# Identity products in TensorE's pauses: 62 at a layer's end, 30 ahead of the norm of the experts

## The chip, the cores and the metric

The kernel runs on one core of a Trainium2 chip. The metric is the device time of one execution in microseconds (us), as the median over runs. The core has TensorE (PE, matrix products into PSUM banks), VectorE (DVE), ScalarE (ACT) and GpSimd (POOL), each with a queue of its own that it works off in order, and SyncE (SP), which issues most of the loads. Engines wait for each other on semaphores. PE's clock is granted in one of two levels, 1.2 and 2.4 GHz; the profile gives it as a share of full speed (PEclk).

## What is computed

The reference is one inference step of a diffusion backbone with two layers, over two groups of tokens with shared weights: 128 context tokens and 256 latent tokens, D = 1024. Cut to what matters here:

```python
def trunk_layer(x, cond, lp_norm, lp_mix, lp_moe, ctx, lam_init):
    mod = jax.nn.silu(cond) @ w_mod_l + b_mod_l
    sh1, sc1, g1, sh2, sc2, g2 = jnp.split(mod[..., None, :], 6, axis=-1)
    h = rmsnorm(x, norm_mix_l) * (1.0 + sc1) + sh1
    y, new = mixer_sublayer(h, lp_mix, ctx, lam_init)   # four mixers, gated merge, output projection
    x = x + g1 * y
    h = rmsnorm(x, norm_ffn_l) * (1.0 + sc2) + sh2
    x = x + g2 * hier_moe(h, *lp_moe)                   # top-1 group of 4, top-2 of its 4 experts
    return x, new
```

After the two layers comes a last rmsnorm. All weights and tokens are float32.

## The kernel before

The 384 tokens stand in three tiles of 128. Each engine has its own instruction stream, and each stream holds one loop over the two layers (`with pe.Fori(0, DEPTH) as l`), whose body walks a list of steps written out ahead of time (SCHEDULE). A layer is: the norm ("norm", 0) with the first units of the input projection; the units of the projections, with the steps of the mixers laid between them; the output projection (wout); the norm of the experts ("norm", 1); the router ("route"); and the experts ("experts"), a loop over six tiles of sorted tokens.

Weights come in units of 512 KB (128 x 1024 f32) through a ring of raw buffers. Each unit is split into a high and a low part in fp32r (whi by ACT, wlo by DVE or POOL), and every product is made of three: high x high, low x high, high x low (function three, L1271 to L1273). The activations are split the same way into hhi and hlo.

The norm. ACT sums the squares of each tile (L952), POOL makes the reciprocal root (L758, L762), DVE and ACT scale the tokens into xn (L1798, L961). PE then transposes xn column by column, 128 of the 1024 features at a time and three tiles to a column (function columns, L1293), DVE applies the modulation while it reads the bank (L1826), ACT makes the high part (L968), DVE and POOL in turn the low part (L1746, L775). In the norm of the experts PE also transposes the finished columns back (function back, L1335) and ACT stores them in hn (L956). Of the first norm, four columns stand ahead of unit 0 and two each behind units 0 and 1. DVE's stream has the low part of unit 0's weights behind the first column, ahead of the low part of the first column.

Ahead of the norm of the experts PE works a quad (function next_quad, L1230): 32 products that make part of the modulation of the next layer. The second quad stands behind the last column, then the router.

At a layer's end the outputs of the last tile of experts are brought back to the tokens' order (back_to_tokens, L1683) and added to x by DVE (L1746); the next layer's sum of squares waits for that (layer_end).

S, T, G and O are PSUM tensors; S has two banks, S0 and S1. The function free(bank) waits until the last reader of a bank is through; a matmul without a wait of its own starts when PE comes to it.

Of the kernel before, what the change touches and what calls it, by code (L numbers as in the profile page):

```python
# [28 lines left out]
P = 128  # L29
# [62 lines left out]
ROPE_AFTER = (20, 21, 22, 22, 23, 43, 45, 47, 49)  # L92
BIASED = [u for u, (ty, t, j) in enumerate(AU) if ty in "BC" and t < 2]
SMALL = 36
FOUR = ("T0", "T1", "S0", "S1")

# [140 lines left out]
def program(nc, a, out, counts):  # L238

    ctx = ExitStack()  # L240
    with ctx:
        def sb(name, shape, dt=F32):
            return ctx.enter_context(nc.sbuf_tensor(name, shape, dt))
# [44 lines left out]
        cst, nrow = sig[:, 2, :], sig[0:1, 0:2, :]  # L288
        small = sb("small", [P, KD, SMALL])
        smhi = sb("smhi", [P, KD, SMALL], F32R)  # L290
        smlo = sb("smlo", [P, KD, SMALL], F32R)
        pcol = sb("pcol", [P, PCOLS])
# [7 lines left out]
        ident = sb("ident", [P, P])  # L300
# [64 lines left out]
        S = ctx.enter_context(nc.psum_tensor("S", [P, 2, 512], F32))  # L365
# [8 lines left out]
        def rows_bank(i, j):  # L374

            return ("S0", "S1", "S0", "S1")[j] if i == 0 else FOUR[j]

        def psum(name):

            return {"S": S, "T": T}[name[0]][:, int(name[1]), :]  # L380
# [76 lines left out]
        def evacuated(c, t):  # L457
            if CHUNKS[c][0] in ("proj", "gate"):
                return ev_act, TILES * sum(CHUNKS[i][0] in ("proj", "gate") for i in range(c)) + t
            step = 2 if c == CHUNK_NO["wout", 1] else 1  # L460
            return ev_dve, TILES * sum(CHUNKS[i][0] not in ("proj", "gate") for i in range(c)) + step * t
# [5 lines left out]
        def pooled(c, t):  # L467

            n = sum(CHUNKS[i][0] == "wout" or (CHUNKS[i][0] == "branch" and CHUNKS[i][1][0] > 0) for i in range(c))
            return TILES * n + t  # L470
# [414 lines left out]
        def _(act):  # L885
# [6 lines left out]
            with act.Fori(0, DEPTH) as l:  # L892
# [46 lines left out]
                for s in SCHEDULE:  # L939
# [213 lines left out]
                    elif s[0] == "mt":  # L1153
                        c = s[1]
                        act.wait_ge(*mt_pe.at(l, c))
                        mh_act.of(nc.scalar.activation(hhi[:, c, :], psum(FOUR[c % 4])[:, 0:384], ACT.Copy, scale=0.5))
                    elif s == ("route",):
# [63 lines left out]
        def _(pe):  # L1221
# [5 lines left out]
            def next_quad(q, where, signal):  # L1227
                for k in range(KD):
                    for i in range(MQ):
                        mm = nc.tensor.matmul(G[32 * i:32 * i + 32, q // 2, P * (q % 2):P * (q % 2 + 1)], cond[:, k, :],  # L1230
                                              where[MQ * q + i][:, k * P:(k + 1) * P], start=(k == 0), stop=(k == KD - 1))
                        if k == KD - 1:
                            signal(mm)
# [15 lines left out]
            with pe.Fori(0, DEPTH) as l:  # L1249
                passed = {}  # L1250

                def need(s, i):

                    if i > passed.get(s.name, -1):
                        passed[s.name] = i
                        pe.wait_ge(s.handle, s.value(l, i))
# [4 lines left out]
                def free(*banks):  # L1261
                    last = {}
                    for b in banks:
                        if read[b] is not None:
                            sgl, i = read[b]
                            last[sgl.name] = (sgl, max(i, last.get(sgl.name, (sgl, i))[1]))
                    for sgl, i in last.values():
                        need(sgl, i)
# [7 lines left out]
                def quad(q):  # L1276
                    need(nx_in[q], MQ - 1)
                    next_quad(q, home, nx_pe.of)

                def turned(h):  # L1280
# [3 lines left out]
                    nxt_pe.of(next_turned(h))  # L1284
                    read["T0"] = None

                def columns(w, c):

                    b = ("T0", "T1") if w else ("T0", "T1", "S0", "S1")
                    b = b[c % len(b)]  # L1290
                    free(b)
                    for t in range(TILES):
                        mm = nc.tensor.transpose((T if b[0] == "T" else S)[:, int(b[1]), t * P:(t + 1) * P],  # L1293
                                                 xn[:, t, c * P:(c + 1) * P], ident[:, :])
                    nt_pe.of(mm)
                    read[b] = (hf_dve, KD * w + c)

                pe.wait_ge(*yo_act.in_tile(l, 0, 1, -1))
                for s in SCHEDULE:
                    if s[0] == "mod":  # L1300
# [11 lines left out]
                        for k in range(KD):  # L1312
                            for q in range(MQ):
                                mm = nc.tensor.matmul(O[32 * q:32 * q + 32, c0:c0 + P], cond[:, k, :],  # L1314
                                                      raw[:, MODPOS[j - MQ + 1 + q] % RAW, k * P:(k + 1) * P],
                                                      start=(k == 0), stop=(k == KD - 1))
# [11 lines left out]
                    elif s[0] == "norm":  # L1328
# [11 lines left out]
                        if w:  # L1340
                            need(*evacuated(CHUNK_NO["wout", 1], 0))
                            quad(0)
                        need(xn_dve, 2 * w)
                        need(xn_act, w)
                        for c in range(KD if w else 4):
                            columns(w, c)
                            if w and c:
                                back(c - 1)
# [3 lines left out]
                    elif s[0] == "gemm":  # L1352
                        g = s[1]
                        c, i, n = GEMM[g]
                        kind, arg, width, _ = CHUNKS[c]
# [25 lines left out]
                        if g < 2:  # L1381
                            columns(0, 4 + 2 * g)
                            columns(0, 5 + 2 * g)
# [64 lines left out]
                    elif s[0] == "m1":  # L1448
# [6 lines left out]
                                         start=True, stop=True)  # L1455
# [5 lines left out]
                    elif s[0] == "m2":  # L1461
# [5 lines left out]
                        if t < 2:  # L1467
# [6 lines left out]
                            for h in range(4):  # L1474
# [3 lines left out]
                                                 start=True, stop=True)  # L1478
# [111 lines left out]
                    elif s[0] == "mt":  # L1590
                        c = s[1]
                        b = CHUNK_NO["branch", (3, c // 4)]
                        need(ev_pool, pooled(b, 2))
                        t4 = FOUR[c % 4]
                        free(t4)
# [5 lines left out]
                    elif s == ("experts",):  # L1601
# [64 lines left out]
                        for hf in range(2):  # L1666
                            for c in range(4):
                                for t in range(TILES):
                                    mm = nc.tensor.matmul((T[:, 1, :], G[:, 2, :])[hf][:, c * P:(c + 1) * P],
                                                          hn[:, t, (4 * hf + c) * P:(4 * hf + c + 1) * P], sel[:, t, :],  # L1670
                                                          start=(t == 0), stop=(t == TILES - 1))
                            q_t.of(mm)
                        need(gates_dve, 0)
                        for t in range(TILES):
                            mm = nc.tensor.matmul(O[:, 0:GRP], sel[:, t, :], hn[:, t, D:ROW],
                                                  start=(t == 0), stop=(t == TILES - 1))
# [5 lines left out]
                        def back_to_tokens(t, hf, **flags):  # L1682
                            return nc.tensor.matmul(last_bank(t, hf), selT[:, t * P:(t + 1) * P], yo[:, hf * 512:(hf + 1) * 512],  # L1683
                                                    **flags)
# [12 lines left out]
                        for hf in range(2):  # L1697
                            nc.tensor.matmul(last_bank(2, hf), ident[:, :], yacc[:, 2, hf * 512:(hf + 1) * 512],
                                             start=True, stop=False)
                            mm = back_to_tokens(2, hf, start=False, stop=True)  # L1700
                        last_pe.of(mm)

        @block.vector
        def _(dve):
# [24 lines left out]
            with dve.Fori(0, DEPTH) as l:  # L1730
# [41 lines left out]
                for s in SCHEDULE:  # L1772
# [289 lines left out]
                    elif s[0] == "mt":  # L2062
                        c = s[1]
                        dve.wait_ge(*mh_act.at(l, c))
                        ml_dve.of(V.scalar_tensor_tensor(hlo[:, c, :], psum(FOUR[c % 4])[:, 0:384], 0.5, hhi[:, c, :].bitcast(F32),
                                                         ALU.mult, ALU.subtract))
# [145 lines left out]
def _layout(i):  # L2212
# [13 lines left out]
    w = i["w_in"][:, :, o["gates"]:o["gates"] + 16]  # L2226
    small = np.concatenate([w, i["router_group"], i["router_expert"]], 2).reshape(L, KD, P, SMALL).transpose(0, 2, 1, 3)

# [31 lines left out]
def _build(nc, arrays, counts):  # L2260

    a = {k: nc.dram_tensor("in_" + k, v.shape, mybir.dt.from_np(v.dtype), kind="ExternalInput").ap()
         for k, v in arrays.items()}
    a["x_scratch"] = nc.dram_tensor("x_scratch", (TILES, P, D), F32, kind="Internal").ap()
    a["g_scratch"] = nc.dram_tensor("g_scratch", (2, 16, P), F32, kind="Internal").ap()
    out = {k: nc.dram_tensor("out_" + k, s, F32, kind="ExternalOutput").ap() for k, s in _OUTS.items()}
    return program(nc, a, out, counts)
# [18 lines left out]
```

## Time and profile before

| | |
|---|---|
| median of 3 runs | 1812.84 us (1809.8 to 1814.68) |
| the profiled execution | 1811.37 us |
| its span, first to last instruction | 1809.8 us |
| PE, DVE, ACT, POOL busy | 94%, 56%, 48%, 36% |
| mean granted clock | 0.979 |
| first layer ends, second begins (PE) | about 914, 922 us |
| norm of the experts (PE) | 653.85 to 664 and 1537.57 to 1547 us |

The busy share of an engine is an average over the span. A row of a timeline gives the start, the duration and the source line of an instruction or of several merged ones (x6), and in brackets how long its engine had been idle and what ended that. A row of the windows gives for one stretch the busy time of each engine with the number of its instructions, then the granted clock, the share in which the DMA engines were busy, and GB/s.

### The profile page before, as it was taken

The page shows a single profiled execution, that of the slowest core. Times are in us where ns is not written, and L with a number is a line of the kernel's source. Part 1 is how long each engine was busy: PE and PEld are TensorE (multiplying, and loading weights), DVE is VectorE, ACT ScalarE, POOL GpSimd, SP SyncE. Part 2 cuts the span into 40 slices and gives each one's busy share as a digit, 9 for nine tenths or more (in the row PEclk, how much of TensorE's full clock was granted, in tenths as well). Part 3 has the DMA queues.
Part 4 walks back from the last instruction along what each step waited for, and adds up shares of the span by engine and source line. Part 5 has one row for each costly group of instructions (what it writes and reads, how often), then busy time and mean ns, then how long its engine had stood idle before and what let it go on. Part 6 is the DMA issues. An engine that isn't in the chain of part 4 may idle for free.

```text
span 1809.8 us, 31099 instructions
## 1 busy us (share of the span) xinstructions
PE 1698.8 (94%) x10123; PEld 1357.5 (75%) x10123; DVE 1016.0 (56%) x1836; ACT 872.8 (48%) x1499; POOL 656.3 (36%) x416
## 2 busy tenths in 40 slices
PE   5999999998999989999979999899999999899997
PEld 3788877676878867777757888776768787777774
DVE  2126455564453148999950382574644502799997
ACT  2333344444433336877733333444444333478774
POOL 1554543333446722000125455333334665201001
PEclk9999999999999999999989999999999999999998
DMA  9532333332556649999935233342535555799994
GB/s 377 176 104 89 114 123 100 110 123 106 187 187 246 223 152 385 379 374 370 335 128 180 93 103 111 97 132 82 181 118 202 190 203 211 272 395 372 365 360 163
DMA packets 120208, 371.67 MB, mean 205 GB/s; under 512 B 12092, under 2 KB 32124, under 8 KB 120064
## 3 DMA queue, kind: packets, MB, share of 16 engines
q1 hardware_dynamic: 94960, 328.62, 50.0%
q0 software_dynamic: 6624, 24.18, 3.5%
q10 hardware_dynamic: 18480, 17.08, 3.0%
q8 instruction: 74, 1.21, 0.3%
q14 instruction: 70, 0.57, 0.1%
HBM read 345.90 MB, written 23.93 MB: 204 GB/s over the span
## 4 chain that ended last, share of the span: by engine, by line
issue 34%; PE 31%; POOL 20%; DVE 8%; ACT 3%; DMA 2%; SPq 1%; POOLq 0%; DVEq 0%; ACTq 0%
POOL wlo L753 16%; PE G L1271 8%; PE G L1273 7%; PE G L1272 7%; DVE wlo L1746 4%; ACT whi L918 2%; DMA lead<-in_units 1%; PE O L1314 1%; PE G L1230 1%; PE S L1271 1%; PE S L1527 1%; PE S L1273 1%; POOL pB L786 1%; PE S L1272 1%; PE T L1541 1%
## 5 line engine op out<-in xcount | busy, mean ns | idle before, releaser
L753 POOL TENSOR_TENSOR wlo<-raw,whi 128x1024 fp32r<-128x1024 f32 x198 | 477.8, 2419 | 593.1 <-ACT whi L910 593.0
L1271 PE MATMUL G<-whi,hhi 128*128 128x512 f32 (+1 forms) x1440 | 580.2, 403 | 19.0 <-POOL wlo L753 7.2
L1273 PE MATMUL G<-whi,hlo 128*128 128x512 f32 (+1 forms) x1440 | 561.1, 390 | 0.0
L1272 PE MATMUL G<-wlo,hhi 128*128 128x512 f32 (+1 forms) x1440 | 560.6, 389 | 0.0
L1271 PEld LDWEIGHTS G<-whi,hhi 128*128 128x128 f32 x1440 | 272.8, 189 | 97.9 <-DVE wlo L1746 20.3
L1273 PEld LDWEIGHTS G<-whi,hlo 128*128 128x128 f32 x1440 | 272.7, 189 | 58.4
L1272 PEld LDWEIGHTS G<-wlo,hhi 128*128 128x128 f32 x1440 | 273.4, 190 | 48.8
L910 ACT ACTIVATE whi<-raw 128x1024 fp32r<-128x1024 f32 x204 | 214.3, 1054 | 153.5 <-DMA raw<-in_units 77.1
L1746 DVE TENSOR_TENSOR wlo<-raw,whi 128x1024 fp32r<-128x1024 f32 x150 | 179.2, 1219 | 5.4 <-ACT whi L918 4.7
L918 ACT ACTIVATE whi<-raw 128x1024 fp32r<-128x1024 f32 x144 | 152.7, 1060 | 29.0 <-PE G L1273 19.7
L1746 DVE TENSOR_TENSOR wlo<-pA,whi 128x1024 fp32r<-128x1024 f32 x72 | 87.7, 1222 | 20.1 <-ACT whi L918 18.3
L1104 ACT ACTIVATE prob<-prob,am 128x384 f32<-128x384 f32 x64 | 38.9, 609 | 114.2 <-DVE am L1746 60.5
L918 ACT ACTIVATE whi<-pA 128x1024 fp32r<-128x1024 f32 x72 | 76.0, 1061 | 31.1 <-PE S L1273 18.7
L1746 DVE TENSOR_TENSOR wlo<-pB,whi 128x1024 fp32r<-128x1024 f32 x72 | 85.1, 1222 | 6.9 <-ACT whi L918 6.3
L1271 PE MATMUL S<-whi,ehi 128*128 128x512 f32 x192 | 79.2, 412 | 3.3 <-DVE elo L1746 3.1
L918 ACT ACTIVATE whi<-pB 128x1024 fp32r<-128x1024 f32 x72 | 75.1, 1057 | 12.7 <-PE G L1273 12.4
L1271 PE MATMUL G<-whi,bhi 128*128 128x512 f32 x192 | 79.7, 415 | 0.0
L1272 PE MATMUL G<-wlo,bhi 128*128 128x512 f32 x192 | 76.6, 399 | 0.0
L1273 PE MATMUL G<-whi,blo 128*128 128x512 f32 x192 | 76.4, 398 | 0.0
L1273 PE MATMUL S<-whi,elo 128*128 128x512 f32 x192 | 75.3, 392 | 0.0
L1272 PE MATMUL S<-wlo,ehi 128*128 128x512 f32 x192 | 75.0, 391 | 0.0
L748 POOL TENSOR_TENSOR sink_col<-ones 128x1 f32<-128x1 f32 x26 | 13.3, 510 | 156.7 <-ACT yo L1206 76.7
(381 smaller groups left out, 2473.1 us busy)
## 6 DMA issues: line engine op xcount, KB each, us to landing
raw<-in_units SPq DMA_DIRECT2D x424, 512.0 KB, 5.2
pB<-in_units SPq DMA_DIRECT2D x75, 512.0 KB, 6.4
pA<-in_units SPq DMA_DIRECT2D x75, 512.0 KB, 6.1
h_sorted<-sig POOLq DMA_DIRECT2D x12, 514.0 KB, 6.9
hs<-h_sorted POOLq DMA_DIRECT2D x10, 514.0 KB, 7.4
kT<-in_units SPq DMA_DIRECT2D x10, 512.0 KB, 4.9
spare<-in_units SPq DMA_DIRECT2D x10, 512.0 KB, 8.1
y_sorted<-yo POOLq DMA_DIRECT2D x10, 512.0 KB, 7.0
```

The lines of the kernel that those rows point to most:

```text
L753: lo_done.of(nc.gpsimd.tensor_tensor(wlo[:, k, :], raw[:, POS_OF[g] % RAW, :], whi[:, k, :].bitcast(F32), ALU.subtract))
L786: ev_pool.of(nc.gpsimd.tensor_tensor(merged[arg[1]][:, t, :], merged[arg[1]][:, t, :], sig[:, t, :], ALU.add))
L910: hi_done.of(nc.scalar.activation(whi[:, g % CONV, :], raw[:, p % RAW, :], ACT.Copy))
L918: hi_done.of(nc.scalar.activation(whi[:, n % CONV, :], expert_raw(n), ACT.Copy))
L1104: e = nc.scalar.activation(prob[:, u % 2, m, 0:w], src, ACT.Exp, bias=am[:, u % 2, m:m + 1], accum_out=am[:, u % 2, 2 + m:3 + m])
L1230: mm = nc.tensor.matmul(G[32 * i:32 * i + 32, q // 2, P * (q % 2):P * (q % 2 + 1)], cond[:, k, :], where[MQ * q + i][:, k * P:(k + 1) * P] ...
L1271: nc.tensor.matmul(dst, st_hi, mv_hi, start=start, stop=False)
L1272: nc.tensor.matmul(dst, st_hi, mv_lo, start=False, stop=False)
L1273: return nc.tensor.matmul(dst, st_lo, mv_hi, start=False, stop=stop)
L1314: mm = nc.tensor.matmul(O[32 * q:32 * q + 32, c0:c0 + P], cond[:, k, :], raw[:, MODPOS[j - MQ + 1 + q] % RAW, k * P:(k + 1) * P], start=(k ...
L1527: nc.tensor.matmul(S[:, m, 0:256], q, kT[r, kj, 0:256], start=True, stop=True)
L1746: return V.tensor_tensor(o, i0, i1, op)
```

## The change

A function keep_busy(n) issues n products of the identity (128x128, f32) with itself into the first 128 columns of bank S0, each a group of its own (start and stop), with no wait and no signal. Nothing reads them. It is called with 30 behind the first quad and ahead of the waits of the norm of the experts, after a free("S0"), and with 62 as the last thing of PE's loop body, behind the last products of the layer.

```diff
+BUSY_END, BUSY_NORM = 62, 30
...
+                def keep_busy(n):
+
+                    for _ in range(n):
+                        nc.tensor.matmul(S[:, 0, 0:P], ident[:, :], ident[:, :], start=True, stop=True)
...
                         if w:
                             need(*evacuated(CHUNK_NO["wout", 1], 0))
                             quad(0)
+                            free("S0")
+                            keep_busy(BUSY_NORM)
                         need(xn_dve, 2 * w)
                         need(xn_act, w)
                         for c in range(KD if w else 4):
...
                             mm = back_to_tokens(2, hf, start=False, stop=True)
                         last_pe.of(mm)
+                        keep_busy(BUSY_END)
```

## Rows read from the trace of the kernel before

**Rows 1.** The page's busy times, with share of the span and instructions.
```profile
PE 1698.8 (94%) x10123; PEld 1357.5 (75%) x10123; DVE 1016.0 (56%) x1836; ACT 872.8 (48%) x1499; POOL 656.3 (36%) x416
```
**Rows 2.** PE's groups by form: shapes, records, then busy us, mean ns, idle before.
```profile
L1397 PE MATMUL O<-ident,prob 16*128 16x16 f32 x12 | 1.7, 261 | 1.1 <-ACT prob L937 1.1
```
**Rows 3.** PE's timeline, gather of the first tile: start us, duration us, what.
```profile
677.62 2.84 PE L1669 MATMUL T<-prob,hn 128*128 128x128 f32 x24
680.30 2.84 PE L1669 MATMUL G<-prob,hn 128*128 128x128 f32 x24
```
**Rows 4.** PE's timeline, first layer's end and second layer's start.
```profile
913.59 1.02 PE L1683 MATMUL O<-yo,prob 128*128 128x512 f32 x2
922.06 1.54 PE L1293 MATMUL T<-ident,pB 128*128 128x128 f32 x6 [7.45 <-ACT pB L961]
...
926.29 0.79 PE L1271 MATMUL G<-whi,hhi 128*128 128x512 f32 x1 [1.41 <-DVE hlo L1746]
...
932.23 0.82 PE L1293 MATMUL T<-ident,pB 128*128 128x128 f32 x6
...
945.56 0.49 PE L1271 MATMUL G<-whi,hhi 128*128 128x512 f32 x1 [3.62 <-POOL wlo L753]
```
**Rows 5.** Windows there: busy by engine, then granted clock, DMA share, GB/s.
```profile
918.50:920.00 1.50, 0.00 (x0) 0.00 (x0) 0.18 (x1) 0.22 (x2) 1.09 (x2) 0.92 1.01 407
...
929.00:930.50 1.50, 1.50 (x6) 1.20 (x5) 1.50 (x2) 0.00 (x0) 1.50 (x1) 0.66 0.25 101
...
947.00:948.50 1.50, 1.50 (x5) 1.17 (x5) 0.00 (x0) 1.18 (x2) 0.77 (x1) 0.52 0.76 298
```
**Rows 6.** Timelines of DVE and POOL, second layer's start.
```profile
923.00 0.86 DVE L1826 TENSOR_SCALAR probT<-T,acol,modc 128x256 f32<-128x256 f32 x2 [1.91 <-PE T L1293]
...
925.69 0.55 DVE L1746 TENSOR_TENSOR hlo<-probT,hhi 128x384 fp32r<-128x384 f32 x1
...
926.47 1.02 POOL L775 TENSOR_TENSOR hlo<-probT,hhi 128x384 fp32r<-128x384 f32 x1 [6.68 <-ACT hhi L968]
...
943.09 4.68 POOL L753 TENSOR_TENSOR wlo<-raw,whi 128x1024 fp32r<-128x1024 f32 x2 [2.10 <-ACT whi L910]
```
**Rows 7.** PE's timeline, norm of the experts, first layer.
```profile
650.02 0.27 PE L1230 MATMUL G<-spare,cond 128*32 128x128 f32 x1
653.85 1.54 PE L1293 MATMUL T<-ident,pB 128*128 128x128 f32 x6 [3.56 <-DVE pB L1798]
...
664.46 0.30 PE L1230 MATMUL G<-spare,cond 128*32 128x128 f32 x1
```
**Rows 8.** Windows, norm of the experts, first layer and second layer.
```profile
653.00:654.00 1.00, 0.15 (x1) 0.15 (x2) 0.79 (x2) 0.53 (x1) 0.00 (x0) 0.76 0.96 340
...
660.00:661.00 1.00, 1.00 (x8) 0.79 (x7) 0.88 (x3) 0.63 (x2) 0.86 (x1) 0.82 0.00 0
...
1541.00:1542.00 1.00, 0.77 (x7) 0.53 (x6) 0.99 (x3) 0.18 (x2) 0.85 (x1) 1.00 0.20 82
```
**Rows 9.** Timelines of PE and DVE, norm of the experts, second layer.
```profile
1533.73 0.27 PE L1230 MATMUL G<-spare,cond 128*32 128x128 f32 x1
1537.57 1.54 PE L1293 MATMUL T<-ident,pB 128*128 128x128 f32 x6 [3.57 <-DVE pB L1798]
...
1547.47 0.30 PE L1230 MATMUL G<-spare,cond 128*32 128x128 f32 x1
...
1543.03 1.67 DVE L1826 TENSOR_SCALAR probT<-T,acol,modc 128x256 f32<-128x256 f32 x4
...
1545.09 1.63 DVE L1826 TENSOR_SCALAR probT<-T,acol,modc 128x256 f32<-128x256 f32 x4
```
**Rows 10.** Waits of SP's queue, experts of the first layer: total us, times, longest.
```profile
SPq L655 <- DVE wlo L1746: 117.2, 122, 3.5
```
**Rows 11.** PE's last product, and a window near the span's end.
```profile
1796.56 1.02 PE L1683 MATMUL O<-yo,prob 128*128 128x512 f32 x2
...
1808.00:1809.00 1.00, 0.00 (x0) 0.00 (x0) 0.00 (x0) 0.00 (x0) 0.00 (x0) 0.50 0.84 336
```

## The prediction

> **What bounds the kernel now.** I read the page first: TensorE (PE) is busy in 94% of the span [rows 1], so a microsecond taken from or given to PE outside its pauses is a microsecond of the kernel. The windows then give the granted clock. It is 0.979 in the mean, 1.00 (2.4 GHz) nearly everywhere, and falls to 0.50 (1.2 GHz) after PE has paused: at a layer's end [rows 5], ahead of the norm of the experts [rows 8], and once more after a pause in which PE waits for GpSimd [rows 4, 5]. Last I read PE's and VectorE's (DVE's) timelines around the two edited places, for what the pause waits for and what follows. The question of the whole case is one of fit: how long are the pauses, and how long are the added products?
>
> **Length of one product.** The operands of the identity products are plain f32, 128 columns, not in transpose form. The trace has this shape elsewhere: the 12 products that gather rows into bank T are 24 matmul records, and the next 24 begin 2.68 us after the first [rows 3]. So one product is two records, 2.68/24 = 0.1117 us apart, 0.223 us in all, at clock 1.00. That a moving identity does not shorten it is seen where the identity is the moving operand of a plain product: 6 products (3 tiles, 2 layers) of 16 columns left 12 records [rows 2]. 62 products are 62 x 0.2233 = 13.85 us, 30 are 6.70 us. Neither batch waits for anything that is still under way, so each starts where the product ahead of it ends, and everything behind it in PE's order starts after it.
>
> The Trainium skill (TensorE: Matmul & The Clock Gate, "Back-to-back issue gap") gives about N/2.4 + 2.5 ns for a product of N columns at the full clock, that is 56 ns at 128. By it the 62 would be an estimated 3.5 us and the 30 an estimated 1.7 us, and both would lie inside the pauses with no lateness. The trace has 0.223 us for this f32 shape and decides.
>
> **Layer end, first to second layer.** PE's last product is two records from 913.59, 0.43 apart as their 512 columns make them, so it clears PE at 914.45; the next work, transposes of the normalised tokens, starts at 922.06 after 7.45 us of idle [rows 4]. The pause is 7.6 us, the batch 13.85: it ends at 928.30, and the transposes start 6.24 us late. What is won back:
> - The three transposes of the first column run at the full clock, 0.32 instead of 0.64 us. DVE begins 0.94 us after them now (923.00) [rows 6], 0.60 then: 928.90.
> - From there to the low part of the first column, which the first product of the layer waits for, is DVE's own chain, 923.00 to 926.24 = 3.24 us [rows 6]. PE then starts unit 0 at 932.15 instead of 926.29 [rows 4].
> - Unit 0 takes 5.94 us now, until 932.23 [rows 4]. The clock is 0.50 until about 930.0 (0.66 over 929.00 to 930.50) [rows 5], so 3.7 us run at half speed: 1.85 are won, 4.1 us remain. Against that, its second column's low part, GpSimd's, ends 1.25 us after the first's (927.49 against 926.24) [rows 6]; a cold PE hardly sees this, a warm one gets there after about 0.8 and waits some 0.5 us. Unit 0 ends at 932.15 + 4.1 + 0.5 = 936.8.
>
> Lateness left: 936.8 - 932.2 = **4.6 us**. It stays. The next pause (3.62 us, until 945.56) is ended by GpSimd's split of unit 3 [rows 4], which waits for ScalarE [rows 6], which by program order comes behind the last columns, and these are transposed by PE behind unit 1: the whole chain moves with PE, and the clock falls after it as now [rows 5]. The bound from below is 2.8 us (all other parts as now, the cold loss of 1.85 in full and no 0.5, and 1.3 us more from DVE's chain, whose last wait on ScalarE may go); from above 6.24, and up to 1 us more if PE's jump back to the loop's start, hidden in the pause now, becomes visible behind the batch. The trace does not show such a jump by itself.
>
> **Norm of the experts, twice.** The 30 stand behind the first quad of the modulation, whose last four start at 650.02 and clear PE at 650.12 [rows 7]. The batch ends at 656.82; the transposes start at 653.85 now [rows 7]. 3.0 us late. Then the clock: now it is 0.50 until about 660.4 [rows 8] and the columns go at PE's cold pace; warm, DVE sets the pace. In the second layer it is back at 1.00 from 1541.0 [rows 8], and DVE then starts a pair of columns every 2.06 us (1543.03 to 1545.09) [rows 9]. A warm stage is: 0.62 us from the transposes to DVE, three pairs at 2.06, and 2.38 us from the last pair's start to the next quad (1545.09 to 1547.47) [rows 9]: 9.2 us. Layer 1: 656.82 + 9.2 = 666.0 against 664.46 [rows 7], **+1.5**. Layer 2: quad clear at 1533.84, batch until 1540.54, quad at 1549.7 against 1547.47 [rows 9], **+2.3**. Together 3.8 us; bounds 2.5 (DVE's pace a tenth better) and 6.0 (nothing won back by the clock). Behind it stand the router, one serial chain at clock 1.00, and the experts, where the queue of the loads waits for DVE, 117 us in 122 waits [rows 10], and so is not what they wait for; no slack takes this up.
>
> **End of the kernel.** The loop's body holds the 62 in the last layer too. The last product starts at 1796.56 (two records, 0.43 apart) and clears at 1797.42 [rows 11]; 13.85 more, and 0.16 for the last record's tail, is 1811.4. The output's transfers still run in the window before 1809.0 [rows 11], and the span ends at 1809.8. PE, idle now, becomes the last engine to finish: **+1.6 us**; bounds 0 and 1.8.
>
> **Sum.** 4.6 + 3.8 + 1.6 = +10.0 us. The profiled execution took 1811.4 us (span 1809.8 and 1.6 around it): 1821.4. The median of the runs is 1812.8, 1.5 above it: 1822.8. I say 1822. With the bounds: 2.8 + 2.5 + 0 = 5.3 to 6.24 + 1 + 6.0 + 1.8 = 15, that is 1817 to 1828.
>
> **Rivals.**
> - *A product costs one record, 0.112 us* (as a transpose does, or because the weights are the same and PE skips a pass). Then the 62 end at 914.45 + 6.9 = 921.4 and the 30 at 653.5, both just inside the pauses, the transposes start on time and warm: layer end -0.3 for the first column and -1.85 +0.5 for unit 0 = -1.7; norms 9.2 against 10.6 and 9.9 = -1.4 and -0.7; the end free. Sum -3.8: 1808 to 1809. It decides from the product's length alone. For it: a transpose streams 128 f32 columns too and is one record (6 for two columns of three tiles [rows 4]), and no row shows a plain product of the identity with itself. Against: the plain products in rows 2 and 3 all have two. 1 in 10.
> - *The lateness is absorbed by the 3.62 us pause before 945.56*, if GpSimd's split doesn't depend on PE. Then the pause shrinks by 3.6 and the fall of the clock behind it goes too (0.52 from 947.0 [rows 5]; if it lasts as long as the 3.7 us of unit 0, 1.8): 10.0 - 5.4 = +4.6, 1817. Against: the order of ScalarE's queue described above. 7 in 100.
> - *Identity products don't hold the clock.* It would fall as now: at 919.8 (0.92 over 918.50 to 920.00 [rows 5]), 5.3 us into the long batch, and at 653.5 (0.76 over 653.00 to 654.00 [rows 8]), 3.4 into the short one; the rest goes at half speed, 0.447 each. 38 of the 62 are then 17.0 us, and the layer end is 14.8 us late; 15 of the 30 are 6.7 us, twice 6.3 late; the last batch, with a fall after 3.4, would end 12 us behind the span. Sum +39, 1850. Against: the clock rose at 660.4 after PE had run only transposes against the identity since 653.85 [rows 7, 8]. 4 in 100.
>
> **Chances.** The forecast has 79 in 100, the rivals 10, 7 and 4. A measurement of this kernel tells 0.3%, 5.4 us, from no change. Slower takes 75 of the forecast's 79, the cold rival's 4 and 1 of the absorbed one's 7: 0.80. Same takes the forecast's lowest edge (3), 6 of the absorbed one (at +0.3%) and 6 of the half-length one (at -0.2%): 0.15. Faster has the other 4 of that one and 1 for what I don't see: 0.05. The range 1815 to 1828 leaves out the half-length and the cold rival and some 5 of the forecast.
>
> **What would show it.** In the changed trace: 124 records behind 914.4 and 60 behind 650.1, 0.112 us apart (62 and 30 records would prove the first rival); clock 1.00 from 905 to the pause before 950 and from 640 to 670; the first transposes of the second layer behind the batch with no idle ahead of them, 13.9 us after the layer's last product instead of 7.6; PE's last record after the output's transfers. The forecast is wrong if the transposes still wait for DVE or ScalarE after the batch, or if the pause before the fourth unit has shrunk.

## The result, and the profile after

| | before | changed |
|---|---|---|
| median of 14 runs each | 1812.55 us | 1824.18 us |
| lowest, highest | 1809.76, 1816.85 | 1817.12, 1830.74 |
| ratio to the kernel before | | 1.0066 [1.0053, 1.0080] |
| the profiled execution, its span | 1811.4, 1809.8 us | 1824.5, 1822.9 us |
| mean granted clock of it | 0.979 | 0.985 |

The changed kernel is 0.66% slower, 11.6 us in the medians. The forecast was 1822, 1815 to 1828. The mean clock went up and so did the time, which is the whole case in two numbers. "Warm" is said of PE where the granted clock is 1.00, "cold" where it is 0.50. Lines of the changed kernel are numbered anew: the products are L1291, function columns L1299, back L1341, the bringing back of the tokens L1691, three L1272 to L1274.

PE's timeline of the changed kernel at the first layer's end (it answers to [rows 4]; start us, duration us, what, and in brackets PE's idle time ahead of it and what ended it):

```profile
909.86 1.02 PE L1691 MATMUL O<-yo,prob 128*128 128x512 f32 x2
910.72 14.01 PE L1291 MATMUL S<-ident 128*128 128x128 f32 x124
926.40 0.87 PE L1299 MATMUL T<-ident,pB 128*128 128x128 f32 x6 [1.68 <-issue]
...
930.27 0.53 PE L1272 MATMUL G<-whi,hhi 128*128 128x512 f32 x1 [2.35 <-DVE hlo L1755]
...
931.52 0.80 PE L1272 MATMUL G<-whi,hhi 128*128 128x512 f32 x1 [0.26 <-POOL hlo L776]
...
936.55 0.82 PE L1299 MATMUL T<-ident,pB 128*128 128x128 f32 x6
```

The batch is 124 records, 0.1117 us apart. Behind it lie 1.68 us that nothing in the profile explains ("issue"), and then 2.35 us in which PE waits for DVE. The windows of that stretch (busy time of PE, its weight loads, DVE, ACT and POOL, then granted clock, DMA share, GB/s) show that the clock still falls, from 931.3 to 934.7:

```profile
925.00:926.00 1.00, 0.00 (x0) 0.00 (x0) 0.00 (x0) 0.00 (x0) 0.00 (x0) 1.00 0.00 0
...
931.00:932.00 1.00, 0.74 (x3) 0.48 (x2) 1.00 (x3) 0.73 (x2) 0.47 (x1) 0.64 0.97 381
932.00:933.00 1.00, 1.00 (x4) 0.71 (x4) 1.00 (x2) 0.32 (x1) 0.54 (x1) 0.50 1.01 414
...
934.00:935.00 1.00, 1.00 (x5) 0.76 (x4) 0.50 (x1) 0.00 (x0) 1.00 (x1) 0.65 0.48 66
```

The norm of the experts in the second layer (it answers to [rows 9]), PE's timeline:

```profile
1542.88 6.96 PE L1291 MATMUL S<-ident 128*128 128x128 f32 x60
1549.69 0.82 PE L1299 MATMUL T<-ident,pB 128*128 128x128 f32 x6
...
1558.69 0.30 PE L1231 MATMUL G<-spare,cond 128*32 128x128 f32 x1
```

The kernel's end (it answers to [rows 11]): the last batch and the last transfers, from the timeline of all engines; the batch ends at 1822.7 and the span at 1822.9.

```profile
1808.65 14.01 PE L1291 MATMUL S<-ident 128*128 128x128 f32 x124
...
1815.36 2.72 SPq L717 DMA_DIRECT2D out_tokens<-pB  x3
```

Cut at the same events, the two traces compare so. "Clear" is the end of the last useful product ahead of a batch: for the narrow quads their last start + 0.11, for the layer's end the last start of a pair + 0.86. Below, the fourth row is called the boundary, the last one the tail, and the two rows of the norm the norm stages.

| stretch, us | before | changed | difference |
|---|---|---|---|
| start to the first quad clear, layer 1 | 650.1 | 644.8 | -5.3 |
| norm of the experts, layer 1, to the second quad | 14.3 | 15.9 | +1.6 |
| router and experts, layer 1 | 250.0 | 250.0 | 0 |
| layer's last product to the end of unit 0 | 17.8 | 25.8 | +8.0 |
| mixers of layer 2, to the first quad clear | 601.6 | 606.2 | +4.6 |
| norm of the experts, layer 2 | 13.6 | 15.9 | +2.3 |
| router and experts, layer 2 | 250.0 | 250.0 | 0 |
| last product to the span's end | 12.4 | 14.3 | +1.9 |

The four stretches that hold a batch add up to +13.8. The two long ones that hold none, -5.3 and +4.6, are the scatter of this kernel: in them the clock falls behind other pauses, mostly for 3.4 or 6.8 us at a time, from trace to trace in other places. In the ten traces of this case in which nothing is changed in it the first stretch took 644.5 to 654.0 us, so a single trace says nothing of a few microseconds of the whole. A part of it shows that this is the clock: from PE's first transposes of the first mixer's rows to the start of the quad ahead of the norm of the experts, the same ten traces took 374.7 us with 7.8 us of it cold, 376.5 with 12.6, 378.1 with 16.0, 379.4 with 19.4 and 381.6 with 22.8. The stretches around an edit repeat within 0.1 us where the clock does not change in them.

### The profile page after: what moved, and what is told of

Its sections match the earlier page's. It is cut to its first block, busy times and chain, and to the rows that moved or that the text cites. A ratio compares the mean times of both kernels' runs of the same rounds, so it can differ in the third digit from the quotient of the medians.

```text
span 1822.9 us, 31835 instructions
## 1 busy us (share of the span) xinstructions
PE 1731.4 (95%) x10491; PEld 1391.7 (76%) x10491; DVE 1010.1 (55%) x1836; ACT 873.0 (48%) x1499; POOL 656.2 (36%) x416
## 4 chain that ended last, share of the span: by engine, by line
PE 51%; issue 19%; DVE 11%; POOL 10%; ACT 4%; DMA 2%; SPq 1%; DVEq 0%; ACTq 0%; POOLq 0%
PE G L1272 12%; PE G L1274 11%; PE G L1273 11%; POOL wlo L754 8%; DVE wlo L1755 4%; ACT whi L919 2%; PE S L1291 2%; PE O L1320 2%; PE S L1535 1%; PE T L1549 1%; PE S L1272 1%; PE G L1231 1%; PE O L1579 1%; DMA lead<-in_units 1%; PE S L1274 1%
## 5 line engine op out<-in xcount | busy, mean ns | idle before, releaser
L1272 PE MATMUL G<-whi,hhi 128*128 128x512 f32 (+1 forms) x1440 | 581.3, 404 | 20.9 <-POOL wlo L754 7.2
L1274 PE MATMUL G<-whi,hlo 128*128 128x512 f32 (+1 forms) x1440 | 561.4, 390 | 0.0
L1272 PEld LDWEIGHTS G<-whi,hhi 128*128 128x128 f32 x1440 | 273.2, 190 | 99.9 <-DVE wlo L1755 20.5
L1274 PEld LDWEIGHTS G<-whi,hlo 128*128 128x128 f32 x1440 | 272.8, 189 | 58.8
L1272 PE MATMUL S<-whi,ehi 128*128 128x512 f32 x192 | 79.0, 412 | 3.2 <-DVE elo L1755 3.1
L1272 PE MATMUL G<-whi,bhi 128*128 128x512 f32 x192 | 78.6, 409 | 0.0
L1274 PE MATMUL G<-whi,blo 128*128 128x512 f32 x192 | 75.4, 393 | 0.0
L1274 PE MATMUL S<-whi,elo 128*128 128x512 f32 x192 | 75.2, 392 | 0.0
L843 POOL TENSOR_TENSOR gate<-hs,ones 128x4 f32<-128x4 f32 x10 | 7.1, 706 | 175.1 <-PE G L1643 175.1
```

Of the source, the lines that this page charges most:

```text
L1272: nc.tensor.matmul(dst, st_hi, mv_hi, start=start, stop=False)
L1274: return nc.tensor.matmul(dst, st_lo, mv_hi, start=False, stop=stop)
```

## Experiments

Theory: a batch costs by its length against the pause that it stands in, and what it outlasts the pause by is paid. Rivals: that batches cost otherwise (by the instruction stream, by moving the falls of the clock), or that identity products don't hold the clock.

**1, 2. Each batch alone.**

```diff
-BUSY_END, BUSY_NORM = 62, 30
+BUSY_END, BUSY_NORM = 0, 30      # experiment 1
+BUSY_END, BUSY_NORM = 62, 0      # experiment 2
```

> The 62 products at the layer's end are left out, the 30 ahead of the norm of the experts stay. Theory (the batch is longer than the pause and only its overhang, less what a warm clock gives back, is paid): the changed kernel's trace has +1.5 us in the first layer's norm stage (15.87 us from the end of the first quad to the second quad, against 14.34) and +2.3 in the second's (15.90 against 13.63), so +3.8 us in all, ratio about 1.002. Rival 1 (the batches cost by what they do to the rest, a longer instruction stream or clock falls elsewhere): the norm stages are the same as in the changed kernel but the whole is off the +3.8 by several us. Rival 2 (the norm batch is neutral, all of the loss is at the layer's end): ratio 1.000.

Measured: 1.0035 [1.0023, 1.0047]. The norm stages are 15.90 and 15.89 us, just as in the changed kernel; so +3.8 in these two. The interval (4.2 to 8.5 us) lies above that; this comparison does not say where the rest comes from, so rival 1 is neither shown nor excluded by it. The boundary of its trace was 1.1 us shorter than before, by a shorter cold stretch. Rival 2 falls.

> The 30 products ahead of the norm of the experts are left out, the 62 stay. Theory: the layer's boundary costs what the changed kernel's trace shows, +8.0 us from the last product of the first layer to the end of unit 0 of the second (25.8 us against 17.8), of which about 1.7 are idle time behind the batch, PE's jump to the loop's start; and +1.9 at the end of the kernel. Sum +9.9, ratio about 1.0055, and with the norm batch alone it adds up to the changed kernel's +11.6 to +13.7. Rival (the 1.7 us of idle behind the batch was chance, and so was the fall of the clock in unit 0): +4.6 and +1.6 as forecast, 6.2, ratio 1.0034.

Measured: 1.0060 [1.0036, 1.0083]. Boundary 26.3 us, with 2.07 us of idle behind the batch, and the fall of the clock again in unit 0; tail 14.3. So neither was chance, and the rival falls. Both batches alone add up to 1.0095, more than the two together (1.0066), but the intervals cover that.

**3, 4. Shorter batches, and transposes in place of products.**

```diff
+BUSY_END, BUSY_NORM = 24, 15     # experiment 3
...
-    nc.tensor.matmul(S[:, 0, 0:P], ident[:, :], ident[:, :], start=True, stop=True)
+    nc.tensor.transpose(S[:, 0, 0:P], ident[:, :], ident[:, :])   # experiment 4, counts 62 and 30
```

> 24 products at the layer's end and 15 ahead of the norm: 24 x 0.2233 = 5.4 us and 1.7 of jump are 7.1, inside the 7.6 us pause; 15 are 3.35, inside the 3.7. Theory (length against pause decides): the transposes start as early as in the kernel before, the norm stages run warm (9.2 us instead of 10.6 and 9.9, -2.1 together), the end of the kernel is free, and the layer's start gains 0 to 1.9 by a warm unit 0 if the clock holds over the short idle stretches behind the batch. Sum -2 to -4, ratio 0.998 to 0.999. Rival (products in a pause cost in themselves, by the stream or by the clock later): ratio 1.000 or above.

Measured: 0.9998 [0.9983, 1.0014]. The norm stages are 12.8 us in both layers (-1.6 and -0.8), the tail is free (12.4). But the boundary is 20.4 us against 17.8. PE's timeline of experiment 3:

```profile
913.93 1.02 PE L1691 MATMUL O<-yo,prob 128*128 128x512 f32 x2
914.79 5.52 PE L1291 MATMUL S<-ident 128*128 128x128 f32 x48
924.59 1.54 PE L1299 MATMUL T<-ident,pB 128*128 128x128 f32 x6 [4.29 <-issue]
```

The batch is over 5.5 us after the last useful product, the tokens are ready at 7.6, and PE starts at 9.8. The expectation, 1.7 us of jump behind the batch, was wrong: the jump costs more behind a short batch. The 2.6 us that the boundary is longer eat the 2.4 us of the norm stages, and the -2 to -4 us expected of the whole did not come.

> The same counts, 62 and 30, but each is a transpose of the identity (one record of about 0.107 us) instead of a product (two records). Theory (length decides, and a transpose keeps the clock as a product does): 62 are 6.6 us and 1.7 of jump, 0.7 us longer than the pause; 30 are 3.2, inside theirs; the end of the kernel is free. -2.1 from the norms, +0.7 - 0 to 1.9 at the boundary: sum -3 to -1, ratio 0.998 to 0.9995. Rival (transposes don't keep the clock): the clock falls in the batches as it does in the pause before, about 5.3 us and 3.4 us into them, the rest goes at half speed: at most 12 transposes more at 0.213 in the first, none in the second; the norm stages are cold as before, ratio 1.000 to 1.001.

Measured: 1.0016 [1.0001, 1.0031]. The norm stages are 12.8 us and warm, so transposes hold the clock there; that rival falls, though the ratio is the one that it gave. The ratio that the theory gave, 0.998 to 0.9995, was missed: the boundary is 21.8 us, 4.0 longer than before, where 0.7 at most was expected. The 62 transposes took 6.9 us, and PE started 11.1 us after the layer's last product:

```profile
912.83 6.93 PE L1291 MATMUL S<-ident 128*128 128x128 f32 x62
923.96 1.54 PE L1299 MATMUL T<-ident,pB 128*128 128x128 f32 x6 [4.20 <-issue]
```

Experiments 3 and 4 have batches that fit the pause and still start the layer late. What they share with the changed kernel is many instructions (a product is two matmuls and two weight loads, a transpose one of each: 96 and 124 here, 248 in the changed kernel), ahead of the jump to the loop's start.

**5. The same time in few instructions.**

```diff
+def keep_busy_wide(n):
+    for _ in range(n):
+        nc.tensor.matmul(S[:, 0, :], ident[:, :], ident[:, :].unsqueeze(1).to_broadcast([P, 4, P]),
+                         start=True, stop=True)
...
+BUSY_END, BUSY_NORM = 6, 15
...
-                        keep_busy(BUSY_END)
+                        keep_busy_wide(BUSY_END)
```

> At the layer's end 6 products of 512 columns instead of the 24 of 128 (6 x 0.86 = 5.2 us against 5.4, 12 matmul records against 48), 15 of 128 ahead of the norm as before. In the run with 24 and 15 the transposes of the second layer came 9.8 us after the layer's last product though their data were there after 7.6, and 4.3 us of idle lay behind the batch. Theory (the jump to the loop's start and the fetch behind it are delayed by the number of instructions that stand ahead of them): with few instructions the transposes start at +7.6 to 8.0 us as before, ratio 0.998 to 0.999. Rival (the delay goes by the length of the batch in time): +9.5 to 9.8 us again, ratio 1.000.

Measured: 0.9987 [0.9975, 0.9999].

```profile
915.80 1.02 PE L1702 MATMUL O<-yo,prob 128*128 128x512 f32 x2
916.66 5.31 PE L1296 MATMUL S<-ident 128*128 128x512 f32 x12
924.28 1.11 PE L1310 MATMUL T<-ident,pB 128*128 128x128 f32 x6 [2.31 <-ACT pB L962]
```

The batch is as long as that of experiment 3 (5.3 against 5.5 us) and has a quarter of its instructions, and the transposes start at 7.62 us, at once when ACT has the tokens ready. So, between these two, the delay goes by instructions and not by time. The boundary is 17.3 us; the clock fell in it at 924.8 for 6.8 us.

**6 to 9. Batches that fit, in the pauses where the clock falls.** All have 15 ahead of the norm; experiments 8 and 9 also have the 6 wide products of experiment 5 at the layer's end, 6 and 7 have none there.

```diff
 # ahead of unit 3 (experiments 7, 8, 9: 15), into bank O
+                        if g == 3:
+                            keep_busy_o(BUSY_UNIT3)
                         need(lo_done, g)
 # behind the first four columns of a layer (experiments 8, 9: 5), into bank O
+                        if not w:
+                            keep_busy_o(BUSY_UNIT0)
 # ahead of the transposes of the first mixer's rows (experiment 9: 18)
+                        b = rows_bank(i, j)
+                        if (i, j) == (0, 0):
+                            free(b)
+                            keep_busy(BUSY_TO)
                         need(hn_dve, 3 * i + 2)
```

> Only the 15 products ahead of the norm of the experts. Theory: norm stages of 12.8 us in both layers against 14.3 and 13.6, the boundary as in the kernel before (17.8 us, or 16.7 where the clock happens to rise earlier), sum -2.4, ratio 0.9987. Rival (a batch that fits gains nothing, since the clock falls elsewhere in its place): 1.000.

Measured: 0.9994 [0.9983, 1.0004]; norm stages 12.8 in both layers, boundary 18.3 (the clock was down for 13.7 us from 915.7). -2.4 in these two stages is shown by the trace; that it reaches the whole is within the interval, and so is no change. Inconclusive between the two.

> 15 products ahead of the norm of the experts and 15 ahead of unit 3 of each layer, whose pause is 3.6 us (into bank O); none at the layer's end. Theory: norms -2.4; behind unit 3's pause the clock was 0.50 for 3.4 us (kernel before) to 6.8 us (changed kernel, second layer), so half of it, 1.7 to 3.4 us in each of the two layers, is won if the clock holds: sum -5 to -8, ratio 0.996 to 0.997. Rival (the fall behind unit 3 is only moved, since what PE did ahead of it, at the layer's start, counts too): the same cold stretch a few microseconds later, ratio 0.9987.

Measured: 0.9946 [0.9927, 0.9964], 1800.77 us. Here is the stretch from about 1.5 us behind the pause of unit 3, second layer, in windows: first the kernel before (the pause ends at 945.56), then experiment 7 (it ends at 936.46).

```profile
947.00:949.00 2.00, 2.00 (x6) 1.57 (x6) 0.00 (x0) 1.54 (x2) 0.83 (x2) 0.52 0.63 244
949.00:951.00 2.00, 2.00 (x7) 1.52 (x7) 0.00 (x0) 0.60 (x1) 2.00 (x1) 0.63 0.80 254
```

```profile
938.00:940.00 2.00, 2.00 (x10) 1.63 (x9) 0.00 (x0) 1.78 (x3) 0.84 (x2) 1.00 0.70 227
940.00:942.00 2.00, 2.00 (x10) 1.68 (x9) 0.00 (x0) 1.37 (x3) 2.00 (x1) 1.00 0.70 244
```

In four microseconds PE does 20 products instead of 13. The fall is not moved to a place nearby, in the first layer neither (60 to 62: 1.00 instead of 0.50), so the rival falls. The gain, 6.5 to 13.2 us, is at the upper end of what was expected or above it. In this trace the clock also stayed up near 438, 517 and 1227, where it fell in the kernel before and where the edit changes nothing; so how much of the gain belongs to unit 3 is not shown.

> The wide batch of 6 at the layer's end, 15 ahead of the norm, 5 ahead of unit 0 (1.1 us of its 1.4 to 2.3 of idle) and 15 ahead of unit 3. Theory: no cold stretch from the layer's end to beyond unit 3; against the run without the batch at the layer's end unit 0 is warm too, -1.9 more: sum -7 to -10, ratio 0.9945 to 0.996. Rival (the jump's delay behind the batch at the layer's end eats it): the boundary is 2 us longer, ratio 0.997 to 0.998.

Measured: 0.9938 [0.9925, 0.9951], 1799.62 us. PE starts unit 0 with no idle behind the 5 products, and the boundary is 16.6 us. That is no better than in experiment 7, 16.6 too, without a batch at the end: in both traces the clock fell ahead of unit 0 (916.0 to 919.4 here, 910.3 to 917.1 there) and was back for it. The expectation that no cold stretch would be left there was wrong. The intervals of 7 and 8 overlap, so what the batch at the layer's end is worth by itself stays open.

> As the run that holds the clock everywhere, and 18 more products (4.0 us) in the 4.5 us pause ahead of the transposes of the first mixer's rows, which wait for VectorE; behind it the clock was 0.50 for 6.8 us in both layers in nearly every trace so far. Theory: both cold stretches go, 3.4 us each: ratio to the kernel before 0.990 (the run without these 18 had 0.9938). Rival (the work behind this pause is not PE's own bound, or the fall is only moved): 0.9938 again.

Measured: 0.9911 [0.9893, 0.9929], 1796.58 us, the fastest of the case. The pause, first in the kernel before, then in experiment 9:

```profile
263.58 0.82 PE L1445 MATMUL T<-ident,pB 128*128 128x128 f32 x6
268.90 1.54 PE L1580 MATMUL S<-ident,pA 128*128 128x128 f32 x6 [4.51 <-DVE pA L1746]
```

```profile
262.87 4.18 PE L1291 MATMUL S<-ident 128*128 128x128 f32 x36
267.58 0.87 PE L1606 MATMUL S<-ident,pA 128*128 128x128 f32 x6 [0.53 <-DVE pA L1773]
```

and the clock behind it, 0.50 in the kernel before and 1.00 here:

```profile
271.00:273.00 2.00, 2.00 (x6) 1.52 (x6) 0.56 (x1) 0.92 (x1) 1.00 (x1) 0.50 0.00 0
```

```profile
271.00:273.00 2.00, 2.00 (x13) 1.65 (x11) 0.00 (x0) 0.08 (x1) 1.45 (x1) 1.00 0.00 0
```

In the second layer the clock stayed up behind this pause as well. But what these 18 products are worth to the whole is not shown: the intervals of experiments 8 and 9 touch (0.9925 to 0.9929), and in the second layer of this trace, whose run was the slowest of its six (1802.64), the clock fell elsewhere. From the pause to the start of the quad ahead of the norm it was down for 13.6 us and PE took 376.7 us; in the kernel before it was down for 12.9 and PE took 376.0.

**10. The changed kernel's lengths in few instructions:** 16 wide products at the layer's end, 30 narrow ones ahead of the norm.

> The changed kernel with its two lengths in time, but the batch at the layer's end as 16 products of 512 columns (13.7 us, 32 records) instead of 62 of 128 (13.85 us, 124 records). Theory (the 1.7 to 2.1 us of idle behind the batch come from the number of instructions ahead of the jump): the transposes start at the batch's end, 13.8 to 14.0 us after the layer's last product instead of 15.7 to 16.1, and the boundary is 1.8 us or more shorter than the changed kernel's 25.8; norm stages 15.9 as there; 1.6 us at the end of the kernel; ratio about 1.005 to 1.0055. Rival (any batch that outlasts the pause exposes the jump): transposes at 15.5 or later.

Measured: 1.0051 [1.0032, 1.0071].

```profile
917.83 13.90 PE L1296 MATMUL S<-ident 128*128 128x512 f32 x32
931.56 0.82 PE L1310 MATMUL T<-ident,pB 128*128 128x128 f32 x6
```

The transposes follow the batch at once, 13.7 us after the layer's last product; boundary 23.6 us, 2.3 less than in the changed kernel. The 1.7 us behind the batch are thus the price of the many instructions. That is a reading of the traces: the ratios, 1.0051 and 1.0066, have intervals that overlap. Here too the clock falls in unit 0 (from 935.9).

**11. A longer batch:** 93 at the layer's end.

> 93 products at the layer's end instead of 62, 30 ahead of the norm as in the changed kernel. Theory (every product beyond the pause is paid in full, 0.2233 us): 31 x 0.2233 = 6.9 us more ahead of the second layer's transposes (22.6 us after the layer's last product against 15.7), and 6.9 more behind the last product of the kernel: 21.2 us of tail against 14.3. Rival (part of the batch runs beside something else): less than 6 in one of the places.

Measured: one run, 1841.7 us. The transposes start 22.5 us after the layer's last product, 6.8 more than in the changed kernel, and the tail is 21.2, 6.9 more:

```profile
915.45 20.93 PE L1291 MATMUL S<-ident 128*128 128x128 f32 x186
937.98 0.87 PE L1299 MATMUL T<-ident,pB 128*128 128x128 f32 x6 [1.60 <-issue]
```

Beyond the pause every added product is paid in full in both places; the whole was timed once only.

```profile
q8 instruction: 74, 1.21, 0.3%
q8 instruction: 78, 1.28, 0.3%
```

Around the layer's boundary this queue shows each time a pair of transfers of 16 KB, 3.1 to 3.5 us apart from start to start. Against the end of the first of the pair (all times in us after the layer's last product):

| run (instructions of filler at the layer's end) | first transfer ends | transposes start | between |
|---|---|---|---|
| before (none) | -5.0 | 7.6, with their data | 12.6 |
| experiment 5 (24) | -0.1 | 7.6, with their data | 7.7 |
| experiment 10 (64) | 9.1 | 13.7, with the batch's end | 4.7 |
| experiment 3 (96) | 8.1 | 9.8 | 1.8 |
| experiment 4 (124) | 9.3 | 11.1 | 1.8 |
| changed kernel (248) | 13.8 | 15.7 | 1.9 |
| experiment 2 (248) | 14.3 | 16.1 | 1.7 |
| experiment 11 (372) | 20.7 | 22.5 | 1.8 |

In all five runs with unexplained idle time the transposes start 1.7 to 1.9 us after this transfer has ended; in the three without it, that moment had passed before their data came or the batch was through. So the idle time behind the batch is, by this timing, a wait for instructions. With batches of one length in time, more instructions ahead of the jump make them come later: -0.1 against 8.1 us (24 and 96 in 5.3 and 5.5 us), 9.1 against 13.8 (64 and 248 in 13.7 and 13.85 us). The count is not all: 64 over 13.7 us have them later than 96 over 5.5 us.

## Why the prediction was right, and what it missed

- **Length of a product.** Right to the last digit given: 124 and 60 records 0.1117 us apart, which makes the batches 13.85 and 6.7 us. The rival of one record per product is out. The 56 ns worked out from the formula of the Trainium skill (TensorE: Matmul & The Clock Gate, "Back-to-back issue gap"), which that section calls the gap of an isolated product, does not hold for this f32 shape: the measured 0.223 us does.
- **The norm of the experts.** Forecast +1.5 and +2.3, measured +1.6 and +2.3. DVE does set the pace once PE is warm; the stage from the batch's end to the second quad is 9.0 us (1549.69 to 1558.69), forecast 9.2.
- **The end of the kernel.** Forecast +1.6, measured +1.9.
- **The layer's end.** Forecast +4.6, measured +8.0 (8.5 in experiment 2), above the stated upper bound of 7.2. The start of the transposes was to be 13.9 us after the last product and was 15.7: the jump to the loop's start, which I had as a possible 1 us and took at nothing, is 1.7 behind this batch. From the transposes to unit 0 it took 3.87 us, forecast 3.85, and the wait for GpSimd's low part is there as well (0.26 us). The step that failed is "3.7 us run at half speed: 1.85 are won". None was won: the clock, held through the batch, fell at 931.3, after PE had been idle for 1.68 us, worked 1.5, been idle for another 2.35 and worked 1.0, and stayed down for 3.4 us, nearly the 3.7 of before; unit 0 took 6.28 us instead of 4.6. So the term is 4.6 + 1.8 + 1.7 = 8.1. Experiments 2, 10 and 11 show the same fall, experiment 10 without the idle time of the jump. A warm unit 0 takes 4.8 us, but it came about by chance too: in experiments 1 and 7, with no batch there, and in 8, the clock had fallen earlier and was back in time. Only in experiment 9, with a wide batch of 5.3 us and 5 products in the second gap, was the whole boundary warm (16.3 us against 16.6 to 16.7 in those three). Why the clock fell in unit 0 with so short gaps ahead of it stays open beyond these rows.
- **The 3.6 us pause ahead of unit 3** keeps its length (3.59), as forecast, against the rival that absorbs the lateness there. The clock fell behind it for 6.8 us instead of 3.4 in this trace, which belongs to the scatter.
- **The sum** was +10.0 and the medians give +11.6. The trace's own stages give +13.8. That the forecast came out 2 us low and not 4 is due to scatter, not to the argument. The total stayed in the range although the layer's end left its own bounds, since the range adds the upper bounds of all terms. Its lower edge, 1815, lies 2 us below the 1817 that the bounds give, for no stated reason.

What stays open: what calls for the instructions behind the jump, and when. The transposes could start no sooner than about 7.6 us after the layer's last product, when their data come. They started at 7.6 with no batch and behind 24 instructions of wide products; at 9.8 behind 96 instructions, at 11.1 behind 124, at 15.7 to 16.1 behind 248 (1.7 to 2.1 after the batch) and at 22.5 behind 372 (1.6 after); behind 64 in 13.7 us, with no idle. The runs show the dependence on the count, and the transfers of queue 8 show what PE waits for; why a transfer starts when it does, they do not show.

## What to carry to other kernels

Before filling a pause, take the length of one filler from a row of the same shape and type (here 0.223 us, two records) and the length of the pause at each place: a batch that fits can win back half of a cold stretch (experiments 7 to 9, with two to five places filled: 0.5 to 0.9%); what outlasts the pause is paid, less what a warm clock gives back, and in the last iteration too. The pauses worth filling are the ones of a few microseconds right ahead of long work that PE bounds. Ahead of a loop's jump use few wide instructions, since many small ones delay what stands behind the jump.

## What the runs showed of the hardware that was not expected

- The jump back of PE's loop over a layer is hidden in a pause of 7.6 us, but with 96 or 124 instructions of filler ahead of it PE stood still for 4.3 and 4.2 us, 2.2 and 3.5 us beyond the time at which its data were ready. The transposes came 1.8 us after a transfer of instructions had ended (8.1 and 9.3 us after the layer's last product).
- Transposes of the identity held the clock through the pause ahead of the norm as products did: 12.8 us stages in experiments 3 and 4 alike.
- Pauses of 3.6 to 7.5 us end in cold stretches of 3.4 to 13.7 us; with all five places of experiment 9 filled, three of them pauses that the change under study left alone, the kernel was 0.89% faster.
- The kernel's scatter from run to run is in good part the clock: the stretch ahead of the first norm of the experts took 644.5 to 654.0 us in ten traces, with the cold stretches in it at other places and of other lengths each time, and in its later part 15 us more of cold time went with 6.9 us more of time. The fastest of the changed kernel's 14 runs (1817.12) had a mean clock of 0.989, the slowest (1830.74) 0.978.
